# Map stage entered after gathered row 151 instead of 160, with one unit search in five pieces inside it

## The reference

```python
def peer_mixer(h, wq, subkeys, u, v):
    q = (h @ wq).reshape(B, S, PEER_HEADS, 2, PEER_HALF_DIM)
    scores = einsum('bshcd,hcnd->bshcn', q, subkeys)
    s_top, i_top = top_k(scores, 16)                      # 16 of 128 keys, twice
    cand = s_top[..., 0, :, None] + s_top[..., 1, None, :]  # 16 x 16 sums
    best, pos = top_k(cand, 16)                           # 16 experts per token and head
    gates = softmax(best)
    # per token: a = h . u[expert];  out = sum gelu(a) * gate * v[expert]
```

## Time and profile before

| | us |
|---|---|
| median of 3 runs | 3832.63 |
| lowest, highest | 3827.8, 3834.66 |
| the profiled execution | 3836.13 |
| its span, first to last instruction | 3834.4 |
| PE busy | 3481.5 (91%) |
| DVE busy | 2637.1 (69%) |
| ACT busy | 990.5 (26%) |
| POOL busy | 1386.9 (36%) |

### The profile page before, as it was taken

One profiled execution on the slowest core, in us unless ns is written; L12 is line 12 of the kernel. 1 busy time (PEld: TensorE's weight loads), 2 busy tenths in 40 slices (PEclk: granted clock), 3 DMA queues, 4 the chain that ended last, 5 costly groups with the idle time before them and its releaser, 6 DMA issues.

```text
span 3834.4 us, 50377 instructions
## 1 busy us (share of the span) xinstructions
PE 3481.5 (91%) x13726; PEld 2221.9 (58%) x13726; DVE 2637.1 (69%) x5617; ACT 990.5 (26%) x2151; POOL 1386.9 (36%) x1220
## 2 busy tenths in 40 slices
PE   4998998999957999999979889989997689999997
PEld 2555445777755458874445454457766544688643
DVE  6656116999898677777656640279998977687775
ACT  1333102323354003330023330123333620133100
POOL 0000001544423656566500000044443256656663
PEclk9999999999978999999989999999998899999998
DMA  6322214888756999999952222178876579999997
GB/s 245 133 106 77 79 76 182 303 308 324 288 166 232 399 400 397 358 369 383 392 211 104 99 85 102 51 265 328 318 287 246 184 301 397 403 380 368 388 391 306
DMA packets 274015, 999.71 MB, mean 261 GB/s; under 512 B 31353, under 2 KB 48249, under 8 KB 262785
## 3 DMA queue, kind: packets, MB, share of 16 engines
q0 software_dynamic: 153600, 553.72, 38.2%
q1 hardware_dynamic: 120194, 443.42, 30.7%
HBM read 971.85 MB, written 25.17 MB: 260 GB/s over the span
## 4 chain that ended last, share of the span: by engine, by line
PE 60%; DVE 15%; DMA 8%; issue 8%; DVEq 3%; POOL 2%; ACT 2%; another core or an unknown queue 0%; ACTq 0%; POOLq 0%; SPq 0%
PE ps L607 14%; PE ps L560 13%; PE ps L787 9%; DMA arena<-in_u_dram,idx 6%; PE ps L527 4%; PE ps L550 3%; PE ps L518 3%; PE ps L615 3%; DVE arena L1425 2%; DVE mod L1431 2%; POOL arena L1167 2%; PE ps L495 2%; DVE mod L1445 2%; PE ps L638 1%; DMA arena<-in_v_dram,idx 1%
## 5 line engine op out<-in xcount | busy, mean ns | idle before, releaser
L1167 POOL DMA_INDIRECT arena<-in_u_dram,idx x512 | 655.1, 1279 | 1000.0 <-issue 659.3
L560 PE MATMUL ps<-hT,mod 128*128 128x256 f32 x4096 | 925.8, 379 | 0.0
L607 PE MATMUL ps<-arena 128*128 128x512 f32 x2048 | 884.8, 595 | 7.7 <-DVE arena L1473 4.0
L1167 POOL DMA_INDIRECT arena<-in_v_dram,idx x512 | 635.1, 1240 | 626.6 <-DVE mod L1431 360.9
L560 PEld LDWEIGHTS ps<-hT,mod 128*128 128x128 f32 x4096 | 758.6, 190 | 92.7
L1425 DVE CUSTOM_DVE_ANT_0 arena<-arena 128x1024 f32<-128x1024 f32 x512 | 617.1, 1224 | 239.7 <-DMA arena<-in_u_dram,idx 221.9
L1431 DVE SCALAR_TENSOR_TENSOR mod<-arena,mod 128x1024 f32<-128x1024 f32 x512 | 657.1, 1283 | 136.1 <-DMA arena<-in_v_dram,idx 96.3
L607 PEld LDWEIGHTS ps<-arena 128*128 128x128 f32 x2048 | 390.6, 191 | 499.5 <-issue 499.4
L981 ACT COPY mod<-ps 128x512 f32<-128x512 f32 x512 | 276.2, 590 | 509.9 <-PE ps L550 451.3
L550 PE MATMUL ps<-const,arena 128*128 128x128 f32 x2048 | 269.0, 274 | 10.6 <-ACT mod L981 6.9
L550 PEld LDWEIGHTS ps<-const,arena 128*128 128x128 f32 x2048 | 236.8, 141 | 44.9 <-ACT mod L981 14.7
(11 more groups left out here) (202 smaller groups left out, 3477.0 us busy)
## 6 DMA issues: line engine op xcount, KB each, us to landing
arena<-in_u_dram SPq DMA_DIRECT2D x256, 512.0 KB
arena<-in_v_dram SPq DMA_DIRECT2D x256, 512.0 KB
arena<-in_ada_w_dram SPq DMA_DIRECT2D x56, 1024.0 KB, 5.0
arena<-in_w_qkv_dram SPq DMA_DIRECT2D x48, 512.0 KB, 5.5
arena<-in_w_m_dram SPq DMA_DIRECT2D x16, 1536.0 KB, 6.6
arena<-in_w_q_dram SPq DMA_DIRECT2D x32, 576.0 KB
gate_scratch<-hT SPq DMA_DIRECT2D x64, 256.0 KB
hT<-gate_scratch POOLq DMA_DIRECT2D x128, 128.0 KB
```

What stands on the lines that cost most here:

```text
L560: last = pe.matmul(ps[:, 6 + tile // 2 % 2, tile % 2 * NT:(tile % 2 + 1) * NT], u_turned[:, tile % 2, k * P:(k + 1) * P], hT[:, k, DT0:SEQ ...
L607: last = pe.matmul(ps[:, 2 * c + n, :], act_t[:, e, c * P:(c + 1) * P], stream[:, slot, n * 512:(n + 1) * 512], start=(half == 0 and e == ...
L1167: pool.indirect_dma_start(out=ring[:, r % RING, :], out_offset=None, in_=table, in_offset=bass.IndirectOffsetOnAxis(ap=idx[:, j % 4, k:k + ...
```

## The change

In the map stage the first row is 152 instead of 161. Batches 0 to 7 take the u rows 152 to 159. Batches 8 to 12 take no row, but one piece each of the search of unit 6: the search among the keys, the 256 sums, the search among the sums, the split of the positions with the reading of the picks, and the indices. Batch 13 makes unit 4's coefficients and takes row 160; batches 14 to 31 take rows 161 to 178. Rows 179 to 191 come behind the map stage; before, it took rows 161 to 191, in its first 31 batches. What is computed is the same.

```diff
-G_ROW = 161
-G_END = 192
+G_ROW = 152
+SEARCH_AT = 8
+G_END = 179
...
-            def top_sums(vals):
+            def sums_of_picks():
 
                 dve.tensor_copy(i_top_f, i_top[:, :, :])
                 dve.tensor_tensor(cand, ...)
                 dve.drain()
+
+            def top_sums(vals):
+
+                sums_of_picks()
                 top8([vals], [pos[:, :]], ...)
...
+            def topk_piece(l, j, piece):
+
+                par = j % 2
+                if piece == 0:
+                    top_keys(gsc[:, par, j // 2, :, :])
+                if piece == 1:
+                    sums_of_picks()
+                if piece == 2:
+                    top8([best[:, par, :]], [pos[:, :]], ...)
+                if piece == 3:
+                    split_picks()
+                    read_picks(sel_f)
+                if piece == 4:
+                    pick_rows(l, j)
...
                     if k == 0 and not of_u:
                         gate_rows(l, j)
-                        if j + 2 < UNITS:
+                        if j + 2 < UNITS and n != G_ROW + SEARCH_AT:
                             topk(l, j + 2)
...
                     columns(l, b)
                     if b >= 1:
                         gate_batch(l, b - 1)
-                    rows(l, G_ROW + b, min(G_ROW + b + 1, G_END))
+                    if SEARCH_AT <= b < SEARCH_AT + 5:
+                        topk_piece(l, 6, b - SEARCH_AT)
+                    else:
+                        n = G_ROW + b - (5 if b >= SEARCH_AT + 5 else 0)
+                        rows(l, n, n + 1)
```

More of the change, by code:

```diff
@@ L1410, in gate_rows @@
                 dve.drain()
+            def topk_piece(l, j, piece):
[5 more added lines that the diff above has]
+                if piece == 2:
+                    top8([best[:, par, :]], [pos[:, :]], [cand.rearrange("p a b -> p (a b)")],
+                         [cand_work.rearrange("p a b -> p (a b)")])
+                if piece == 3:
[3 more added lines that the diff above has]
+                    pick_rows(l, j)
             def rows(l, first, end):
```

## The result

| | before | changed |
|---|---|---|
| median of 14 runs each | 3832.65 us | 3845.56 us |
| ratio, 95% interval | | 1.003 [1.0019, 1.004] |
| profiled execution | 3836.13 us | 3853.21 us |
| first maps to first value tile, layer 1 / 2 | 140.4 / 142.3 us | 146.3 / 146.4 us |
| PE's wait at tile 32 of half 1, layer 1 / 2 | 4.02 / 0 us | 14.97 / 14.24 us |

One of the 14 executions before took 4300.97 us; the ratio is that of the fast executions alone. The profiled execution of the changed kernel is the slowest of its 14.

What follows compares the result with a forecast made beforehand. DVE was taken to bound the map stage, and full DMA engines the rows behind it. First layer +2.0 us and second -0.6 us summed to +1.4 us, so 3834.0 us, range 3826 to 3847.

Steps and rivals of the forecast that it cites:

- The entry: Start of the map stage: first maps come 15.1 us sooner in the first layer, 14.5 us in the second.
- The stage: Length of the map stage: 4.5 us more work plus 0.4 us for the risk of short batches.
- The value tiles: Start of the value tiles behind the map stage: 10.2 us sooner in the first layer, 9.6 in the second.
- The thirteen rows: Rows 179 to 191 behind the stage: 27.6 us less 13.6 for the closed hole, 14.0 us late.
- The barrier, first layer: PE at tile 32 of half 1 waits some 16 us for kept maps; the layer ends 2.0 us later.
- The barrier, second layer: Same tile: lateness 14.0 less 7.1 us slack, a wait of about 6 us; layer sum -0.6 us.
- The clock: PE's matmuls after the second layer's new wait: 3.0 us lost to a lower granted clock.
- The end of a layer: From the last row to the reload of x: 16.6 us of room, so nothing lost, bound 3 us per layer.
- The rows' lateness is larger: Rival, slower: at tile 32, lateness of 21 us gives +14 us, 3847; chance 0.19 for lateness above 17 us.
- the rows catch up: Rival, faster: lateness falls to 7 us or less before row 462, -7 to -10 us, 3823 to 3826; chance 0.13.
- Tiles come late: Rival: rows in flight starve the value tiles and PE waits, 2 us per layer, 3838; counted in the 0.60 forecast.
- the stage is much longer: Rival: five batches without rows run into PE and ACT, 5 us more per layer, +10 us, 3844; chance 0.08.

Runs made afterwards that it cites:

- after_13_small: Changed kernel, but POOL loads a plain 64 KB block instead of the 512 KB gather for rows 179 to 191; 3835.92 us, ratio 1.001 to before.
- gap_search: Kernel before, with the stage from row 152, unit 6's search whole before its first wait, rows 152 to 183 inside; 3813.68 us, ratio 0.9959.
- gap_27rows: gap_search with only 27 rows (152 to 178) in the stage and 13 behind it; 3818.28 us, ratio 0.9972 to before.

## Where the prediction held and where it failed

*The entry* (15.1 and 14.5 us sooner): 13.4 on average. The view was right, DVE's order held the stage back, and the new wait is 11.4 us. The term was taken from one profile in which rows 152 to 159 had waited some 2 us longer than in the other two.

*The stage* (4.5 us of work and 0.4 for the risk, 4.9 us longer): 5.5. Right.

*The value tiles* (10.2 and 9.6 us sooner): 7.9. The two small misses add up to 2 us per layer.

*The thirteen rows* (14.0 us late, bounds 8 to 27.6): 14.3. The size was right, in part by luck, since the working does not hold. I priced 13 transfers at 2.13 us and took off 13.6 us for the closed hole. after_13_small showed that without the transfers 11.4 us of the lateness stay. I had written that DVE has the time for its 16 us of rows. It hasn't: all of them stand in front of row 192 and replace only the 3.9 us in which it had waited for ACT, a wait that I had not seen in the hole of the earlier trace rows. The transfers add 5.3 us of waits to the last four rows. The hole in the DMA share of the earlier trace rows closes in large part (0.39 to 0.87); no run shows the 13.6 us that I gave for it. My sign "row 192 three or four us later" followed from that working and was off by 13 us.

*The barrier, first layer* (a wait of some 16 us): 15.0, and 12.2 on average of three. Right in size, though the time given back to the rows during the wait (1.8 us) can't be seen. The 4.0 us before were a sample too: in the other two profiles of before this layer had no wait. On average it grew by 10.8 us, where the term had 12.2.

*The barrier, second layer* (a wait of 6 us, sum -0.6): this step failed. It measured 14.2, 14.7 and 14.9. I had taken a slack of 7.1 us from one execution and set it as the layer's property. In that profile PE had come 3.4 us late to half 1: 1.5 us were lost in the first value matmuls, with a granted clock of 0.66 from 3088 to 3093, and 1.9 between 3390 and 3396, where the profile names no engine that PE waited for. Over the three profiles of before the kept batches end 1 us before PE needs them, in both layers alike. A lateness of 14.3 less 1.0 makes 13.3 us of wait, and 13.4 was measured. So both layers pay as the first did. Put right, the sum is per layer -7.9 for the start, +12.3 for the wait and a rest of +0.4: +4.8, where I had +2.0 and -0.6.

*The clock* (3.0 us lost after the new wait): the 256 matmuls behind the wait took 111.66 and 112.05 us against 110.03, so 1.6 and 2.0 us. The 3.0 us came from the first layer of before, where the same 256 took 113.16 us behind the wait of 4.02, with a granted clock of 0.63 from 1817 to 1825; behind the waits of 2.9 and 2.8 us in gap_search they took 110.12 and 110.13. The stretch behind the wait of the changed kernel, at a granted clock of 0.98:

```profile
1826.00:1926.00 100.00, 100.00 (x230) 44.35 (x231) 61.93 (x69) 0.22 (x1) 64.66 (x45) 0.98 1.00 389
```

*The end of a layer* (nothing): held. From the last value tile of the first layer to row 0 of the second it took 588.7 to 591.0 us before and 587.9 to 591.0 changed.

*The sum.* The forecast was +1.4 us, the stretches of the profiles make +9.6. Of the 8.2 us between, 4.0 are the later start of the value tiles (15.8 us sooner in two layers, not 19.8) and 6.4 the longer waits at tile 32 (24.6 us more, not 18.2); the clock and the rest cost 2.2 less than I had put in.

*The rivals.* "The rows' lateness is larger" was to give the slower side; the lateness was not larger, the slack was smaller. The slower time came by a mis-sized slack and a smaller gain at the entry, a case that I had not listed. The rival "the rows catch up" had a slip in its sum: a lateness of 7 us gives 3.2 + 6.6 us and more, -10 to -13 us and not -7 to -10. "Tiles come late" and "the stage is much longer" didn't happen: PE was busy 184.00 of 184.00 us at a share of 1.01. My estimate by the page of the Trainium skill on DMA: Bandwidth & Descriptors (Where 436 GB/s comes from) had been +14 us (by the terms of the sum a lateness of 20 us gives +12 to +13), near the result, but its ground did not hold: the page has the HBM side bind at about 358 GB/s, and these traces, with one core at work, moved 389 to 407 GB/s over 95 us and more, with a lateness of 14.3 and not 20 us.

*What the change is made of*, by the runs: the earlier entry with the search left out of the stage is worth 15.7 us (gap_search). Five rows fewer in the stage cost 5 (gap_27rows), which the two intervals can't tell from nothing. The search in pieces in the stage costs 22 us by the ratios (changed kernel), 19 by the profiles' stretches. Gains and losses of single parts are known to some 5 us, not better. Eight rows behind the stage make 3.8 us of lateness and thirteen 11 to 15. Most of that stands at row 192 already, which is 5.6 us late with eight: they need 9.2 us of DVE, fill its wait for ACT, and none of them waits for its transfer (gap_search). Eight is the size of the ring, so they can lie there when the stage ends; no run varied the ring. Open is why 2 to 3 us are made up on the way from row 192 to the kept batches in some kernels and almost none in others.

## What to carry to other kernels

When a change lets DVE wait for another engine, look first for work that needs nothing of it, and put that in the wait: here the earlier entry with the search in its wait was worth 0.4%, and the same search cut in pieces into the stage that DVE bounds turned the gain into a loss. Work moved out of a bound stage has to be priced where it lands: if the engines behind it are full, rows that start late stay late, and moving the barrier that shows it brings nothing (or a new wait). A slack read from one profile is a sample; before a term is built on it, take it from several executions or carry its scatter in the range.

## What I had not expected of the hardware

One and the same wait, PE for ACT for DVE in the stage of the queries, was between 1.7 and 13.4 us in executions of the same kernel, and the stage 401 to 417 us, on one core. The part ahead of it scatters too: row 0 began between 627.5 and 635.5 us in the profiles of this study, though no edit touches what stands before it. With the value tiles at full width the DMA engines carried 399 GB/s at a share of 1.01 over 184 us, 91 gathers of 512 KB among it, and PE never waited for a tile; with the tiles at half width the share was still 0.95 to 0.97, as the rows took most of what came free.
